# Other byte offsets in SBUF for the operands of TensorE's matmuls, stage by stage, in a three-layer kernel of one core

## The reference, cut to what matters

```
qkv = norm(x) @ w_qkv          # A: 1024 x 9216, B: 1024 x 3072, C: 1024 x 1536 and some more
x   = x + mixed(qkv) @ w_out   # 1024 x 1024
u   = norm(x) @ w_up           # 1024 x 5632
g   = silu(conv3(u)[:, :2816]) * conv3(u)[:, 2816:]
x   = x + g @ w_down           # 2816 x 1024
```

## The kernel before

| operand | modulo 256 |
|---|---|
| w_raw, w_hi (every slot) | 128 |
| w_lo, QKV (offset 0) | 128 |
| w_lo, FFN up (offset 16 elements) | 192 |
| w_lo, FFN down, output projections, PRE (offset 32 elements) | 0 |
| x of the FFNs, hi and lo | 192 |
| x of QKV and PRE: hi, lo | 192, 64 |
| mix_hi, mix_lo | 64 |
| g_hi, g_lo | 192 |

## Time and profile before

### The profile page before, as it was taken

The page is one execution under the profiler, slowest core; times in us unless marked ns, Lnnn a source line. Parts: engine busy times, 40 slices in busy tenths (PEclk is TensorE's granted clock), DMA queues, the critical chain, the costliest instruction groups (busy, mean ns, idle before and its releaser), DMA issues.

```text
span 1038.5 us, 21191 instructions
## 1 busy us (share of the span) xinstructions
PE 1031.9 (99%) x7496; PEld 961.8 (93%) x7496; DVE 868.3 (84%) x1589; ACT 688.0 (66%) x1264; POOL 354.1 (34%) x370
## 2 busy tenths in 40 slices
...
GB/s 320 227 164 157 144 177 158 147 172 205 161 223 206 208 192 188 179 101 188 154 176 132 189 203 217 196 187 194 157 107 133 162 123 203 207 206 195 199 163 41
DMA packets 57749, 183.34 MB, mean 177 GB/s; under 512 B 6352, under 2 KB 9680, under 8 KB 57424
## 3 DMA queue, kind: packets, MB, share of 16 engines
...
HBM read 181.36 MB, written 1.05 MB: 176 GB/s over the span
## 4 chain that ended last, share of the span: by engine, by line
PE 88%; DVE 9%; DMA 1%; issue 1%; ACT 1%; POOL 0%; DVEq 0%; ACTq 0%; POOLq 0%
PE ps L433 19%; PE ps L435 9%; PE ps L681 9%; PE ps L682 9%; PE ps L683 9%; PE ps L1763 5%; PE ps L1765 5%; PE ps L1764 5%; DVE w_lo L401 4%; PE ps L1239 2%; PE ps L1241 2%; PE ps L1240 2%; DVE xg L498 1%; DVE prob L1822 1%; DMA w_raw<-w_stream 1%; PE ps L859 1%
## 5 line engine op out<-in xcount | busy, mean ns | idle before, releaser
L401 DVE TENSOR_TENSOR w_lo<-w_raw,w_hi 128x1024 fp32r<-128x1024 f32 (+2 forms) x369 | 442.2, 1215 | 32.8 <-ACT w_hi L393 32.0
L393 ACT ACTIVATE w_hi<-w_raw 128x1024 fp32r<-128x1024 f32 (+2 forms) x369 | 353.6, 972 | 125.4 <-PE ps L435 108.5
L433 PE MATMUL ps<-xg,w_hi 128*128 128x512 f32 x1056 | 364.1, 390 | 0.8 <-DVE xg L498 0.6
L435 PE MATMUL ps<-xg,w_lo 128*128 128x256 f32 x1056 | 291.6, 276 | 0.0
L433 PEld LDWEIGHTS ps<-xg,w_hi 128*128 128x128 f32 x1056 | 198.2, 188 | 41.7 <-DVE xg L498 2.9
L435 PEld LDWEIGHTS ps<-xg,w_lo 128*128 128x128 f32 x1056 | 198.2, 188 | 0.1
L1885 POOL TENSOR_TENSOR prob_t<-prob_t,qkT 128x256 f32<-128x256 f32 x63 | 104.5, 1659 | 261.8 <-ACT prob_t L1808 261.8
L681 PE MATMUL ps<-w_hi,xg 128*128 128x384 f32 (+1 forms) x556 | 193.0, 347 | 0.0
L683 PE MATMUL ps<-w_hi,xg 128*128 128x384 f32 (+1 forms) x556 | 186.9, 336 | 0.0
L682 PE MATMUL ps<-w_lo,xg 128*128 128x384 f32 (+1 forms) x556 | 186.4, 335 | 0.0
L1763 PE MATMUL ps<-g_hi,w_hi 128*128 128x256 f32 x528 | 146.1, 277 | 0.8 <-DVE g_lo L1844 0.8
...
## 6 DMA issues: line engine op xcount, KB each, us to landing
...
```

Of the source, the lines that this page charges most:

```text
L393: nc.scalar.activation(w_hi[s][:, 0:w], w_raw[s][:, 0:w], ACT.Copy).then_inc(w_hi_done, 1)
L401: nc.vector.tensor_tensor(w_lo(c)[:, 0:w], w_raw[s][:, 0:w], w_hi[s][:, 0:w].bitcast(F32), ALU.subtract).then_inc(w_lo_done, 1)
L433: nc.tensor.matmul(bank(b, 0, 2 * TOK), w_hi[s][:, k * P:(k + 1) * P], xg[:, k, :, :].rearrange("p h t -> p (h t)"), start=(k == 0), stop= ...
L435: last = nc.tensor.matmul(bank(b), w_lo(c)[:, k * P:(k + 1) * P], xg[:, k, 0, :], start=False, stop=(k == KT - 1), skip_group_check=True)
```

## The change

No instruction, wait or DMA is added or taken away, and no loop is altered. What changes is where in a partition the operands of the matmuls lie.
- A w_lo slot becomes 1056 elements (4224 bytes). `lo_at` takes its offsets from a table by stage: 16, 0, 16 elements for QKV A, B, C; 0, 0, 16 for the output projections; 16 for PRE; 16 for FFN up; 0 for FFN down.
- x has one layout in `xg` for all stages, hi and lo of a tile side by side, and begins at 16 elements, in QKV B at 8.
- mix_hi and mix_lo begin at 16 elements, in layer C mix_lo at 48.
- g_hi and g_lo are cut out of one tensor at an offset of 8 elements.
- `X0` is 64 instead of 16 elements, the unused tensor `gap` is 24 elements, and the six small `fg` tensors stand together.

All other hunks pass the stage's number to reach the right view. The diff, cut to its core:

```diff
--- before.py
+++ after.py
@@ -40,11 +40,13 @@
 WARM_UP = 16
 HALVES = 3
 GAINS = 16
-X0 = GAINS
-GAP = 8
-X_APART = 32
-STAGGER = 64
-LO_QKV, LO_UP, LO_DOWN = 0, 16, 32
+X0 = 64
+GAP = 184
+SHIFT = 32
+X_AT = (16, 16, 8, 16, 16, 16)
+G_AT = ((8, 8), (8, 8), (8, 8))
+MIX_AT = ((16, 16), (16, 16), (16, 48))
+LO_QKV, LO_OUT, LO_PRE, LO_UP, LO_DOWN = (16, 0, 16), (0, 0, 16), 0, 16, 0
 CHUNK = KT * P
 UNIT = 3 * P
 QCHUNK = 2 * UNIT
@@ -76,12 +78,11 @@
 
 
 def lo_at(c):
-
     for f in range(3):
         if c < OUT_C0[f]:
-            return LO_DOWN if f == 2 and c < C_QKV else LO_QKV
+            return LO_PRE if f == 2 and c < C_QKV else LO_QKV[f]
         if c < FFN_C0[f]:
-            return LO_DOWN
+            return LO_OUT[f]
         j = c - FFN_C0[f]
         if j < 3 * FT:
             return LO_DOWN if j >= 6 and j % 3 == 0 or j >= 3 * FT - 2 else LO_UP
@@ -189,22 +190,19 @@
 
     w_raw = [sb(f"w_raw{s}", [P, CHUNK]) for s in range(RING)]
     w_hi = [sb(f"w_hi{s}", [P, CHUNK], F32R) for s in range(RING)]
-    w_low = [sb(f"w_lo{s}", [P, CHUNK + STAGGER], F32R) for s in range(RING)]
+    w_low = [sb(f"w_lo{s}", [P, CHUNK + SHIFT], F32R) for s in range(RING)]
     x_all = sb("x_all", [P, X0 + KT * TOK])
     xT = x_all[:, X0:X0 + KT * TOK].rearrange("p (k t) -> p k t", t=TOK)
-    xg_all = sb("xg", [P, 2 * KT * TOK + X_APART], F32R)
-    xg = xg_all[:, 0:2 * KT * TOK].rearrange("p (k h t) -> p k h t", h=2, t=TOK)
-    xs_hi, xs_lo = [xg_all[:, o:o + KT * TOK].rearrange("p (k t) -> p k t", t=TOK) for o in (0, KT * TOK + X_APART)]
-    xg_hi, xg_lo = (xs_hi, xg[:, :, 0, :]), (xs_lo, xg[:, :, 1, :])
-    mix_hi = sb("mix_hi", [P, KT, TOK], F32R)
-    mix_lo = sb("mix_lo", [P, KT, TOK], F32R)
-    fg_m, fg_e = [sb(f"fg{n}", [P, 2 * HEADS_C]) for n in range(2, 4)]
-    fg_r = sb("fg0", [P, 2 * HEADS_C])
+    xg_all = sb("xg", [P, KT * 2 * TOK + SHIFT], F32R)
+    xg = [xg_all[:, o:o + KT * 2 * TOK].rearrange("p (k h t) -> p k h t", h=2, t=TOK) for o in X_AT]
+    xg_hi, xg_lo = [x[:, :, 0, :] for x in xg], [x[:, :, 1, :] for x in xg]
+    mix_all = [sb(f"mix_{n}", [P, KT * TOK + 2 * SHIFT], F32R) for n in ("hi", "lo")]
+    mix_hi, mix_lo = [[mix_all[n][:, o[n]:o[n] + KT * TOK].rearrange("p (k t) -> p k t", t=TOK) for o in MIX_AT]
+                      for n in range(2)]
     par = sb("par", [P, N_PAR])
     con = sb("con", [P, N_CON])
     zero = sb("zero", [P, TOK], BF16)
-    fg_x = sb("fg1", [P, 2 * HEADS_C])
-    sb("gap", [P, GAP])
+    sb("gap", [P, GAP - 5 * SHIFT])
     ln_x = sb("ln_x", [P, TOK])
     rms_r = sb("rms_r", [P, TOK])
 
@@ -230,7 +228,7 @@
     rot_1 = sb("rot_1", [P, 12, ROPE_DIM])
     rot_2 = sb("rot_2", [P, 12, ROPE_DIM])
     tri = sb("tri", [P, 3 * P], F32R)
-    fg_n, fg_l = [sb(f"fg{n}", [P, 2 * HEADS_C]) for n in range(4, 6)]
+    fg_r, fg_x, fg_m, fg_e, fg_n, fg_l = [sb(f"fg{n}", [P, 2 * HEADS_C]) for n in range(6)]
     fg_hi = sb("fg_hi", [P, 2 * HEADS_C], F32R)
     fg_lo = sb("fg_lo", [P, 2 * HEADS_C], F32R)
 
@@ -238,10 +236,9 @@
     cv_s = [[qkT[b][1][:, s * TOK:(s + 1) * TOK] for s in range(2)] for b in range(2)]
     gate_s, gated = prob_t[:, 0, 0, 0:TOK], prob_t[:, 1, 0, 0:TOK]
     up_sum = [prob[s][:, 0:TOK] for s in range(2)]
-    sb("g_gap", [P, 8])
-    g_hi = [sb(f"g_hi{b}", [P, TOK], F32R) for b in range(2)]
-    g_lo = [sb(f"g_lo{b}", [P, TOK], F32R) for b in range(2)]
-    sb("cv_gap", [P, 24])
+    g_all = sb("g_hi0", [P, 4 * TOK + SHIFT], F32R)
+    g_hi, g_lo = [[[g_all[:, o[n] + (2 * n + b) * TOK:o[n] + (2 * n + b + 1) * TOK] for b in range(2)] for o in G_AT]
+                  for n in range(2)]
 
     cv_a, cv_b, cv_e, cv_acc = [[qkT[n // 2][n % 2][:, (1 + i) * TOK:(2 + i) * TOK] for i in range(2)] for n in range(4)]
     cv_h = [sb(f"cv_h{i}", [P, PADC + TOK + 2]) for i in range(2)]
...
@@ -428,19 +425,19 @@
-    def project2_k(eng, c, b, k):
+    def project2_k(eng, c, e, b, k):
-        nc.tensor.matmul(bank(b, 0, 2 * TOK), w_hi[s][:, k * P:(k + 1) * P], xg[:, k, :, :].rearrange("p h t -> p (h t)"),
+        nc.tensor.matmul(bank(b, 0, 2 * TOK), w_hi[s][:, k * P:(k + 1) * P], xg[e][:, k, :, :].rearrange("p h t -> p (h t)"),
-        last = nc.tensor.matmul(bank(b), w_lo(c)[:, k * P:(k + 1) * P], xg[:, k, 0, :], start=False,
+        last = nc.tensor.matmul(bank(b), w_lo(c)[:, k * P:(k + 1) * P], xg_hi[e][:, k, :], start=False,
-    def project2(eng, c, per, i, b):
+    def project2(eng, c, per, i, e, b):
-            project2_k(eng, c, b, k)
+            project2_k(eng, c, e, b, k)
...
@@ -612,7 +609,7 @@
-                last = nc.tensor.matmul(bank(unit_bank(st, u, t), 0, UNIT), (xs_hi, xs_lo)[x][:, k, t * P:(t + 1) * P],
+                last = nc.tensor.matmul(bank(unit_bank(st, u, t), 0, UNIT), xg[2 * st][:, k, x, t * P:(t + 1) * P],
...
@@ -677,7 +674,7 @@
-                hi, lo = xs_hi[:, k, t * P:(t + 1) * P], xs_lo[:, k, t * P:(t + 1) * P]
+                hi, lo = xg[2 * st][:, k, 0, t * P:(t + 1) * P], xg[2 * st][:, k, 1, t * P:(t + 1) * P]
...
@@ -1236,9 +1233,9 @@
-            nc.tensor.matmul(out_acc(m), wh, mix_hi[:, k, :], start=(idx == 0 and m % 2 == 0), stop=False, skip_group_check=True)
-            nc.tensor.matmul(out_acc(m), wh, mix_lo[:, k, :], start=False, stop=False, skip_group_check=True)
-            last = nc.tensor.matmul(out_acc(m), wl, mix_hi[:, k, :], start=False, stop=(idx == KT - 1), skip_group_check=True)
+            nc.tensor.matmul(out_acc(m), wh, mix_hi[st][:, k, :], start=(idx == 0 and m % 2 == 0), stop=False, skip_group_check=True)
+            nc.tensor.matmul(out_acc(m), wh, mix_lo[st][:, k, :], start=False, stop=False, skip_group_check=True)
+            last = nc.tensor.matmul(out_acc(m), wl, mix_hi[st][:, k, :], start=False, stop=(idx == KT - 1), skip_group_check=True)
...
@@ -1760,9 +1757,9 @@
-                    nc.tensor.matmul(acc(m), wh, g_hi[b][:], start=first, stop=False, skip_group_check=True)
-                    nc.tensor.matmul(acc(m), wh, g_lo[b][:], start=False, stop=False, skip_group_check=True)
-                    last = nc.tensor.matmul(acc(m), wl, g_hi[b][:], start=False, stop=True, skip_group_check=True)
+                    nc.tensor.matmul(acc(m), wh, g_hi[f][b], start=first, stop=False, skip_group_check=True)
+                    nc.tensor.matmul(acc(m), wh, g_lo[f][b], start=False, stop=False, skip_group_check=True)
+                    last = nc.tensor.matmul(acc(m), wl, g_hi[f][b], start=False, stop=True, skip_group_check=True)
...
@@ -2079,14 +2076,14 @@
-            nc.scalar.activation(mix_hi[:, 6 + t, :], bank(Q_BANK, t * TOK), ACT.Copy,
+            nc.scalar.activation(mix_hi[2][:, 6 + t, :], bank(Q_BANK, t * TOK), ACT.Copy,
-            nc.vector.scalar_tensor_tensor(mix_lo[:, 6 + t, :], bank(Q_BANK, t * TOK), par[:, PAR_PSC + t:PAR_PSC + t + 1],
-                                           mix_hi[:, 6 + t, :].bitcast(F32), ALU.mult, ALU.subtract).then_inc(side_lo, 1)
+            nc.vector.scalar_tensor_tensor(mix_lo[2][:, 6 + t, :], bank(Q_BANK, t * TOK), par[:, PAR_PSC + t:PAR_PSC + t + 1],
+                                           mix_hi[2][:, 6 + t, :].bitcast(F32), ALU.mult, ALU.subtract).then_inc(side_lo, 1)
```

More of the change, by code:

```diff
@@ L451, in project_first @@
                 eng.wait_ge(x_lo, KT * e + k + 1)
-                project2_k(eng, c, b0, k) if e % 2 else project_k(eng, c, bank(b0), xs_hi, xs_lo, k)
+                project2_k(eng, c, e, b0, k) if e % 2 else project_k(eng, c, bank(b0), xg_hi[e], xg_lo[e], k)
             if k >= lag:
@@ L457, in project_first @@
                         eng.wait_ge(x_new, KT * (e - 1) + 4)
-                project2_k(eng, c + 1, b1, k - lag) if e % 2 else project_k(eng, c + 1, bank(b1), xs_hi, xs_lo, k - lag)
+                project2_k(eng, c + 1, e, b1, k - lag) if e % 2 else project_k(eng, c + 1, bank(b1), xg_hi[e], xg_lo[e], k - lag)
         if e % 2:
@@ L473, in first_hi_dve @@
         eng.wait_ge(x_first, 16)
-        nc.vector.tensor_scalar(xs_hi[:, 0, :], xT[:, 0, :], norm_gain(0, 0), None, ALU.mult).then_inc(x_hi, 1)
+        nc.vector.tensor_scalar(xg_hi[0][:, 0, :], xT[:, 0, :], norm_gain(0, 0), None, ALU.mult).then_inc(x_hi, 1)
     def resid_act(eng, e, m):
@@ L485, in resid_act @@
                 eng.wait_ge(row_in, 16)
-        nc.scalar.activation(xg_hi[e % 2][:, m, :], xT[:, m, :], ACT.Copy, scale=norm_gain(e, m)).then_inc(x_hi, 1)
+        nc.scalar.activation(xg_hi[e][:, m, :], xT[:, m, :], ACT.Copy, scale=norm_gain(e, m)).then_inc(x_hi, 1)
         if e > 0:
@@ L986, in mix_a_act @@
             eng.wait_ge(a.nm, 4 * (pr + 2) + 2)
-        nc.scalar.activation(mix_place(mix_hi[:, pr, :]), pv_read(pr), ACT.Copy).then_inc(a.ohi, 1)
+        nc.scalar.activation(mix_place(mix_hi[0][:, pr, :]), pv_read(pr), ACT.Copy).then_inc(a.ohi, 1)
     def q_act(eng, st, pr):
@@ L1045, in mix_act @@
         eng.wait_ge(a.pv, pr + 1)
-        nc.scalar.activation(mix_hi[:, pr, :], bank(K_BANK), ACT.Copy).then_inc(a.ohi, 1)
```

(15 more changed lines are left out.)

6 lines of the change are left out of this document (3 added, 3 removed).

## The result

| | before | after |
|---|---|---|
| median, us | 1040.26 (4 runs, 1040.18 to 1040.33) | 1047.05 (4 runs, 1046.88 to 1047.63) |
| profiled execution, us | 1040.33 | 1046.62 |
| its span, us | 1038.5 | 1044.8 |

The ratio is 1.0066, with a 95% interval of 1.0049 to 1.0084. The forecast was 1042.7 with a range up to 1046.0. The direction is right. The size is off by 4.4 us, and the median lies 1 us above the range.

The account below looks back on a forecast made before the run. TensorE was taken to bound the kernel, its time being the sum of distances between matmul starts. Terms 3.6 + 0.9 - 0.6 - 1.5 = +2.4 us on 1040.3 gave 1042.7 us, range 1034.8 to 1046.

Parts of the forecast that it names:

- Part 3: FFN up: odd slots get distance 128 in the 512-column matmul; bound 4.8 us, taken as 0 because it still alternates.
- The fourth case: Rival: FFN up collides as well, 1042.7 plus up to 4.8 us, about 1046; chance 0.12.
- Part 1: FFN down: w_lo in even slots moves to 128, giving distances 64, 64, 64; +3.6 us.
- Part 2: Output projections: 8 of 16 chunks in A and B become 192, 192, 192, +0.9 us; C a few tenths either way.
- the floor: Fastest steady distance between matmul starts: 113.3 ns per 256 columns, 170.0 ns for 384.
- Reading (a): In the matmul pace, distances (moving start minus next stationary start, modulo 256 bytes) must alternate by 128; three equal ones collide.
- Reading (b): Only position modulo 128 counts; moving operand wants 64; PRE suffers as its moving operand jumps by 128 between hi and lo.
- Part 4: PRE: with hi and lo both at 192 and w_lo at 192 or 64, it gives back 0.6 us.
- Part 5: QKV: new places of x and w_lo gain a quarter of the 5.8 us bound, taken as -1.5 us.
- QKV freed: Rival: QKV stages are freed and nothing else is hurt, at most -6.4 us, about 1036; chance 0.36.
- 12 of 12: QKV: 12 of 12 matmuls run above their fastest pace far behind any pause, cited against the rival that addresses don't matter.
- Part 6: The rest: norm, softmax and rope operands, x_all and VectorE's w_lo writes; taken as 0.

Follow-up runs that it names:

- kernel 2: Kernel before, with w_lo of FFN up chunks in odd slots 128 bytes further (at 64 instead of 192 modulo 256): 1047.47 us, ratio 1.0068.
- Kernel 1: Kernel before, with w_lo of FFN down chunks in even slots 128 bytes further (at 128 instead of 0 modulo 256): 1040.38 us, ratio 1.0005.
- kernel 5: Changed kernel, with w_lo of FFN up chunks in odd slots back at 192 instead of 64 modulo 256: 1040.86 us, ratio 1.0005 to the kernel before.
- Kernel 7: Kernel before, with w_lo of the PRE chunks at 128 instead of 0 modulo 256: 1040.07 us.
- kernel 12: Kernel before, with PRE's x hi and lo at 192, its w_lo at 128 or 0, and QKV C's w_lo at 192: 1039.9 us, ratio 0.9997.
- kernel 6: Kernel before, with mix_hi and mix_lo at 192 instead of 64 modulo 256 and w_lo of the output projections at 128 in every slot: 1040.31 us.

## Why the prediction was right in sign and wrong in size

**The method held.** TensorE sets the end, its time is the sum of the distances between starts, and these depend on byte places. The kernel lost 6.3 us of span without one more instruction, and kernel 2 lost as much by moving one operand by 128 bytes in 66 chunks.

**Part 3, FFN up, is the step that failed.** I took 0 of a bound of 4.8 us, "as it still alternates". It measured +4.3 us, 3.8 in odd slots, where w_lo went to 64 and the 512-column matmul has the distance 128, and 0.5 in the even slots behind them. The fourth case, "FFN up collides as well", gave 1046 and had a chance of 0.12. With the terms that I took for the rest it comes nearest to the 1047.05 measured, and 1042.7 + 4.3 is 1047.0. That this fits is luck: QKV was off by +3.4, the pauses by -3.2 and the output projections A and B by -1.0, which nearly cancel.

**Part 1, FFN down, had the amount right (+3.2 of 3.6) for the wrong cause, by luck.** Kernel 1 has exactly the new down places and loses nothing. Kernel 2 has the old down places and loses 1.33 us a layer in them. The pace is inherited from the odd-slot up chunk ahead. Parts 1 and 3 are thus one loss with one cause: kernel 5 undoes the up part alone, and both go.

**Part 2, output projections A and B: +0.9 was -0.1.** 192, 192, 192 in even slots costs nothing there on the whole: the chunk is entered at the floor, or mostly falls back to it. Reading (a), that three equal distances collide, is refuted by kernel 1. Reading (b), that only the position modulo 128 counts, is refuted by kernel 2, since there w_lo moved by exactly 128. In C the surcharge rose by 0.5.

**Part 4, PRE: -0.6 was -0.4.** The direction held, though by other places of w_lo than I had read. They are 64, 64, 64 in even slots and 64, 192, 64 in odd ones. Kernel 7 has only w_lo at 128 and stays above the floor; kernel 12, with both, reaches it. As 64, 64, 64 keeps the pace that it enters with, the odd slots should be what clears it. The timelines of the changed kernel and of kernel 12 agree: the fall to the floor stands inside the chunks of slots 1 and 3 (in slot 3 after four matmuls at 4 to 7 ns over it). No run isolates this step.

**Part 5, QKV: -1.5 was +1.9, the wrong sign.** I assumed that QKV could be freed at all. In the changed kernel and in four kernels with other places no slot came to 170.0, and most places are worse than the old one. The rival "QKV freed" at 0.36 was far too likely: no mean in the rows of before showed 384 columns at the floor, which should have been counted against it. The prediction's "12 of 12" above the floor is such a mean: of those 12 matmuls 8 take 4 to 8 ns more and 4 take 169 or 170 ns.

**Pauses, not predicted: -3.2 us.** The surcharges add up to +9.6; shorter stops give 3.2 back. Of these, 2.2 lie in the first two up chunks of FFN B and C (1.24 and 1.25 us of pauses before, 0.27 and 0.05 after), where TensorE waited for `xg`. A slower TensorE alone doesn't fill them: kernel 2 runs the FFNs as slowly and keeps 1.25 us in each. What differs is VectorE, in the eight steps that write the lo part of x for the FFN. Those of FFN B in the kernel before, kernel 2, kernel 6 and the changed kernel (count, busy us, mean ns):

```profile
L498 DVE SCALAR_TENSOR_TENSOR xg<-x_all,par,xg 128x256 fp32r<-128x256 f32 x8 | 5.6, 712 | 0.2 <-ACT xg L486 0.2
...
L500 DVE SCALAR_TENSOR_TENSOR xg<-x_all,par,xg 128x256 fp32r<-128x256 f32 x8 | 5.6, 710 | 0.2 <-ACT xg L488 0.2
...
L498 DVE SCALAR_TENSOR_TENSOR xg<-x_all,par,xg 128x256 fp32r<-128x256 f32 x8 | 4.8, 601 | 0.3 <-ACT xg L486 0.3
...
L495 DVE SCALAR_TENSOR_TENSOR xg<-x_all,par,xg 128x256 fp32r<-128x256 f32 x8 | 4.9, 619 | 0.3 <-ACT xg L483 0.2
```

All kernels that keep the wait for `xg` have 709 to 713 ns there in FFN B and C, and the three in which it is gone (the changed kernel, 5 and 6) 598 to 619. In kernel 6 no operand of that step has moved, so its place isn't what made it faster. GpSimd works on `tokbuf` beside these steps; whether the way the two fall together decides it isn't shown. This gain also hides the cost of kernel 6 and of QKV in kernel 5.

Part 6, the rest, held in that no wait for VectorE grew anywhere. But it took 0, and VectorE's shorter steps go with those 2.2 us at the starts of the FFNs.

What stays open: what inside the chip makes the pace stick, what lifts it where no place has changed (kernel 1), why the mean of 384 columns never comes to 170.0 (single matmuls do: 30% in QKV A before, 7% after, pauses left out), and whether the distance or each operand's own place counts (only some combinations were run).
